# Expert stage: w_down loaded with four consecutive rows per partition, gate and up products with a column step of four

## What is computed

```python
# 4 groups of 8 experts; each token takes 2 experts of 1 group; D = 1024, D_EXPERT = 512
for g in range(N_GROUPS):
    h = silu(einsum('nd,edf->nef', xt, w_gate[g])) * einsum('nd,edf->nef', xt, w_up[g])
    out = out + einsum('nef,efd->nd', h * combine[:, g, :, None], w_down[g])
```

## Time and profile before

| | |
|---|---|
| median of 3 runs | 1153.3 us (1147.21 to 1155.6) |
| profiled execution | 1153.28 us |
| its span in the profile | 1151.5 us |
| mean granted clock of TensorE | 0.888 |
| PE busy | 907.6 us (79%) |
| DVE busy | 519.8 us (45%) |
| ACT busy | 371.5 us (32%) |
| POOL busy | 201.8 us (18%) |
| packets of the SP queue | 94,269, 297.95 MB |

### The profile page before, as it was taken

The page is one execution under the profiler, slowest core; times in us unless marked ns, Lnnn a source line. Parts: engine busy times, 40 slices in busy tenths (PEclk is TensorE's granted clock), DMA queues, the critical chain, the costliest instruction groups (busy, mean ns, idle before and its releaser), DMA issues.

```text
span 1151.5 us, 18005 instructions
## 1 busy us (share of the span) xinstructions
PE 907.6 (79%) x7832; PEld 738.0 (64%) x7832; DVE 519.8 (45%) x788; ACT 371.5 (32%) x516; POOL 201.8 (18%) x78
## 2 busy tenths in 40 slices
PE   4987486856657574757588599998799988999997
PEld 4987476523334242424254289778799988988986
DVE  5425623421202020202022469999995667553642
ACT  4452410110101010101011444456646544533441
POOL 1022400000000000000000388801236950000000
PEclk8998595987878787979798789999999989999999
DMA  9860370999999999999999645414538634555520
GB/s 355 256 234 1 134 304 1 382 420 423 422 421 422 422 422 421 422 420 421 422 422 422 207 143 183 155 41 149 177 125 268 226 134 152 194 181 185 191 102 36
DMA packets 95042, 299.90 MB, mean 260 GB/s; under 512 B 9181, under 2 KB 45581, under 8 KB 86797
## 3 DMA queue, kind: packets, MB, share of 16 engines
q1 hardware_dynamic: 94269, 297.95, 66.8%
q0 software_dynamic: 576, 1.18, 0.4%
q10 hardware_dynamic: 144, 0.00, 0.0%
HBM read 298.07 MB, written 1.05 MB: 260 GB/s over the span
## 4 chain that ended last, share of the span: by engine, by line
PE 53%; DMA 25%; DVE 15%; ACT 3%; issue 3%; SPq 1%; DVEq 0%; ACTq 0%
DMA mem<-in_w_up 22%; PE PS L1658 12%; PE PS L1659 11%; PE PS L1660 11%; PE PS L1812 8%; DVE PS L1469 6%; PE PS L1825 4%; PE PS L1800 1%; PE PS L1651 1%; DVE ring_rest L1447 1%; DVE mem L1579 1%; DVE HN L1160 1%; DMA mem<-in_w 1%; PE PS L1838 1%; PE PS L1780 1%
## 5 line engine op out<-in xcount | busy, mean ns | idle before, releaser
L1812 PE MATMUL PS<-mem 128*32 128x256 f32 x2048 | 155.6, 471 | 109.6 <-DMA mem<-in_w_up 109.6
L1660 PE MATMUL PS<-HT_hi,ring_rest 128*128 128x256 f32 x752 | 214.1, 285 | 0.0
L1812 PEld LDWEIGHTS PS<-mem 128*32 128x32 f32 x2048 | 83.8, 135 | 183.0 <-issue 161.2
L1660 PEld LDWEIGHTS PS<-HT_hi,ring_rest 128*128 128x128 f32 x752 | 145.2, 193 | 0.0
L1658 PE MATMUL PS<-HT_hi,z_hi 128*128 128x256 f32 x440 | 126.5, 287 | 9.6 <-ACT mem L891 5.8
L1659 PE MATMUL PS<-HT_rest,z_hi 128*128 128x256 f32 x440 | 125.9, 286 | 0.0
L1269 DVE TENSOR_TENSOR mem<-mem,PS 128x128 f32<-128x128 f32 x32 | 9.2, 288 | 236.6 <-ACT mem L785 236.6
L607 POOL TENSOR_TENSOR ring_rest<-mem,z_hi 128x2048 fp32r<-128x2048 f32 x19 | 88.4, 4657 | 101.2 <-DVE ring_rest L1447 83.4
L612 POOL TENSOR_TENSOR ring_rest<-mem,z_hi 128x512 fp32r<-128x512 f32 x4 | 5.9, 1513 | 518.5 <-ACT z_hi L812 518.5
L1586 DVE TENSOR_TENSOR ring_rest<-mem,mlp_hi 128x4096 fp32r<-128x4096 f32 x16 | 70.8, 4424 | 57.6 <-ACT mlp_hi L990 57.6
L1658 PEld LDWEIGHTS PS<-HT_hi,z_hi 128*128 128x128 f32 x440 | 86.0, 195 | 10.6 <-ACT mem L891 6.2
(11 more groups left out here) (344 smaller groups left out, 1933.0 us busy)
## 6 DMA issues: line engine op xcount, KB each, us to landing
mem<-in_w_gate SPq DMA_DIRECT2D x32, 2048.0 KB, 15.3
mem<-in_w_up SPq DMA_DIRECT2D x32, 2048.0 KB, 19.7
mem<-in_w_down SPq DMA_DIRECT2D x32, 2048.0 KB, 11.9
mem<-in_w SPq DMA_DIRECT2D x16, 2048.0 KB, 8.0
mem<-in_w_in SPq DMA_DIRECT2D x28, 1024.0 KB, 5.3
mem<-in_w_in SPq DMA_DIRECT2D x5, 2048.0 KB, 19.6
mem<-in_w_b_out SPq DMA_DIRECT2D x4, 1536.0 KB, 8.8
mem<-in_w_out SPq DMA_DIRECT2D x2, 2048.0 KB, 14.9
```

The costliest lines, as they stand in the source:

```text
L1660: ins = nc.tensor.matmul(dst, s_rest, m_hi, start=False, stop=stop and n == len(terms) - 1, skip_group_check=True)
L1812: ins = nc.tensor.matmul(PS[SLOTS * j:SLOTS * (j + 1), bank, 0:2 * F_STRIP].rearrange("p (w n) -> p w n", w=2), xg[:, k, :], w[:, :, k, F_ ...
```

## The change

`w_down` gets the same layout as gate and up have: partition p holds rows 4p to 4p+3, one contiguous piece of 16 KB. Chunk k of the down product is then the rows 4p + k, so strip k of the hidden features has to be 4n + k, n from 0 to 127. The gate and up products pick these columns out of their weights: the moving operand, 128 neighbouring columns of each matrix before, is now every fourth column from column j on. The number and order of instructions on every engine stay as they were.

```diff
-        wd_d = A["w_down"][0].rearrange("g e (k p) n -> (g e) p k n", p=P)
+        wd_d = A["w_down"][0].rearrange("g e (p k) n -> (g e) p (k n)", k=STRIPS)
...
             def load_down(w, place, signal):
-                sp.dma_start(place.rearrange("p (k n) -> p k n", n=D), wd_d[bass.ds(w, 1)].rearrange("e p k n -> p (e k) n")).then_inc(signal, 16)
+                sp.dma_start(place, wd_d[bass.ds(w, 1)].rearrange("e p n -> p (e n)")).then_inc(signal, 16)
...
                         ins = nc.tensor.matmul(PS[SLOTS * j:SLOTS * (j + 1), bank, 0:2 * F_STRIP].rearrange("p (w n) -> p w n", w=2),
-                                               xg[:, k, :], w[:, :, k, F_STRIP * j:F_STRIP * (j + 1)],
+                                               xg[:, k, :], w[:, :, k, :].rearrange("p w (n j) -> p w j n", j=STRIPS)[:, :, j, :],
                                                start=k == 0, stop=k == KC - 1, tile_position=(0, SLOTS * j))
```

## The result

The changed kernel takes 1186.7 us (median of 4 runs, 1183.92 to 1190.01) against 1154.04 us for the kernel before (4 runs): ratio 1.031, 95% interval 1.0268 to 1.0351. That is 33 us slower, where 5 us faster had been forecast, and above the top of the range.

A forecast was written before the change was run, and what follows sets the result against it. The prediction took weight loads (6 MB per expert) to bound the expert stage until 574.85 us, then PE. 24 down loads saving 0.207 us each and free strided reads gave 1153.3 - 5.0 + 0 = 1148.3 us; 8-in-10 range 1142 to 1173.

The forecast's parts named there:

- The rival of no gain: Third rival, on the w_down loads: larger pieces save nothing, down keeps 5.11 us, kernel 1153.3 us; chance 0.10.
- From this row I take a cost of nothing: Gate and up products: reading every fourth column costs 0, judged from the stationary operand in the turning of X.
- the two rows: Turning of X: eight weight loads at a 32-byte step take 0.97 us together, eight of contiguous rows 0.91 us.
- The one that I feared: Gate and up blocks: four strips reading at once might have to take turns, up to 14.6 us a block.
- The rule of the Trainium skill: SBUF lines are 16 bytes; full bandwidth needs at least two hits per line, so step-16 gate blocks slow down.
- the first rival: Gate and up blocks: strided reads halve their pace, adding 25.6 us in the chain, kernel 1174 us; chance 0.13.
- the five blocks of the tail: Gate blocks at 597.33, 610.25 (two), 623.35 and 640.13, after the DMA-bound stretch: 3.64 us more each, the last about 2.9.
- The start: Two gate blocks in the chain before the DMA-bound stretch, each 3.64 us longer if strided reads halve the pace.
- The loop: DMA-bound stretch, 246.9 to 574.8 us: slower gate blocks stay within 2.3 us of cover; the block at 574.85 gains 0.9.
- A block may grow by 2.3 us before DMA idles: DMA-bound stretch: queue work left at the tightest load, the down load issued at 375.43, covers 2.3 us of growth.
- The four-fold case: Second rival, gate and up blocks: the four strips take turns, 14.6 us a block, kernel about 1340 us; chance 0.06.

## Why the prediction was wrong

**The load: right.** Down loads were to go from 5.107 to 4.90 us; with the pieces alone they take 4.903. The 24 of them save 4.9 us, the stage as a whole became 6.3 us shorter, and the forecast was 5.0. The rival of no gain falls.

**The step that failed: "From this row I take a cost of nothing."** The cost of a moving read at 16 bytes was taken from the two rows. Those are turns, and the operand there is the stationary one. The runs show that turns are the exception: 0.109 to 0.121 us at steps 1 to 8. An ordinary product at the same step takes 0.24 instead of 0.112 us with a stepped stationary operand, and 0.45 instead of 0.22 with a stepped moving one. I had called it the nearest row, but it differed in two ways at once, and I weighed only one (one reader against four). The one that I feared does not exist: four strips are as fast as one. The rule of the Trainium skill, which I set below the row, was right for this operation.

**The mechanism of the first rival was right, at 0.13, and its price too low.** Blocks of 7.3 us, as it said, also after a wait (7.45 us). It came to 1174 us, and the kernel takes 1186.7. By its terms: the five blocks of the tail were put at 17.5 us (four at full clock 14.6, the last 2.9) and measure 17.9. The start was put at 7.3 us, two blocks, and measures 10.5: there all four blocks of pack 0 count. The loop was put at 0.9, for the block at 574.85, the last of pack 6, and measures 10.5. There the step "A block may grow by 2.3 us before DMA idles" failed: it was worked out from one down load in the middle of a pack, while at the boundary the growth of two blocks, 4.8 to 6.0 us, comes ahead of one gate load, and even the down loads with 4.3 us left were late. These shares count from the kernel with the pieces alone: -6.3 + 38.9, and 2.6 us that belong to no single part, make the 35.1 us of the stage, where the rival had -5.0 + 25.6. The 5 us of faster loads, which the rival kept, are in effect lost beside the step: with it the stage takes 485.0 us in 4 KB pieces and 485.2 in 16 KB.

**The range** reached to 1173, where the price of that rival ended, and not to its own uncertainty. The four-fold case at 0.06 has no ground left.

## What to carry to other kernels

For float32 on the moving side, and on the stationary side of a product, let at least two columns fall into each aligned 16 bytes; below that the product takes up to twice as long (0.45 against 0.22 us for 256 moving columns), for one strip as for four. If a layout has to be permuted, put the permutation where it is read least: in the small turn of a 32 x 512 result here (0.33 us more for each expert), rather than in the 4 MB of weights. And before taking the price of an operand from a neighbouring row, check the kind of operation as well as the pattern; a slower block is hidden only as far as the tightest place of the loop allows, which may be a boundary that comes every fourth time.

## What the runs showed of the hardware

- A place of 16 bytes costs a float32 read 1.76 ns and a column 0.85 ns; the larger sum counts (steps 1, 2, 3 and 4: 0.217, 0.227, 0.340 and 0.451 us for 256 columns). Pairs across a border of 16 bytes (0.220 us) cost twice what pairs inside one do (0.112). At step 4 this pace does not depend on the granted clock: in the block at 347.76 of the changed kernel the groups of four follow each other after 0.45 us while the clock is 0.51 and when it is 1.00, so the block takes 7.45 us, and one at full clock 7.3. At step 1 the same groups take 0.427 us at the low clock (in the block at 366.17 of before) and 0.216 at the full one (in the block at 358.46).

```profile
348.00:350.00 2.00, 2.00 (x20) 0.79 (x16) 0.00 (x0) 0.00 (x0) 0.00 (x0) 0.51 0.94 401
350.00:352.00 2.00, 2.00 (x24) 0.87 (x20) 0.00 (x0) 0.00 (x0) 0.00 (x0) 1.00 1.09 467
```

- Turns (transpose mode) read a stationary operand at step 4 or 8 within 11% of step 1 (0.121 and 0.115 us against 0.109). Products do not: 0.233 against 0.112 us with 128 columns, 0.060 against 0.033 for four strips of 32.
- A 2 MB load takes 5.11 us in 4 KB pieces, 4.96 in 8 KB and 4.90 in 16 KB when the queue is full. With only 2.9 to 3.5 us of loads ahead of it at its issue, such a load landed up to 2.3 us late.
